# Final layer norm: weight multiplied during the output product, bias and mean added by a rank-two product

## The chip, the cores and the metric

The kernel runs on one core of a Trainium2 chip. The metric is the device time of one execution in microseconds (us), lower is better. The engines named below are TensorE (PE), VectorE (DVE), ScalarE (ACT), GpSimd (POOL) and the DMA queues that SyncE (SP) and GpSimd issue to.

## What is computed

One layer of a decoder trunk for 512 prompt tokens and 64 sample tokens, 2048 channels, all in float32. Only the last line concerns the change:

```python
def layer_norm(x, g, b):
    mu = jnp.mean(xf, axis=-1, keepdims=True)
    var = jnp.mean(jnp.square(xf - mu), axis=-1, keepdims=True)
    return (xf - mu) * lax.rsqrt(var + LN_EPS) * g + b

def mix_and_norm(x, y_a, o_b, z_b, g_a, g_b, w_o_a, w_o_b, w_out, ln_g, ln_b):
    ...
    return layer_norm(DN_ALPHA * x + merged @ w_out, ln_g, ln_b)
```

Everything before it (the input projection, attention, the gated branch) fills the first 2258 us of the kernel and is the same in both versions.

## The kernel before

The output product works on 16 blocks of 128 channels. For each block PE streams four quarters of the weight (`quarter`, L736, 96 records) into one of two PSUM banks (`acc`). Each quarter was rounded by ACT (`wh`, L942) and split by DVE (`wl`, L1231) two quarters ahead, through a ring of three. ACT then copies the block out (`read_out`, L1184), PE transposes it to tokens by channels (`out_turn`, L923 and L925, into `turn`), DVE adds the scaled input (`residual`, L1655), which fills 128 channels of `res`, and takes the statistics of that block (`statistics`, L1664). `res` holds 5 tiles of tokens: tiles 0 to 3 have 128 rows, tile 4 has the 64 sample rows.

After block 15 nothing but the norm is left. DVE aggregates the statistics (L1685), ACT takes the square root (L1198), DVE the reciprocal (L1689) and `shift`, minus the mean times the reciprocal (L1690). The normalisation itself then runs over ten half tiles of 1024 channels, in an order that is written out by hand. Tiles 0 and 1 are DVE's alone: `centred` (L1706, subtract the mean and multiply with the weight `lng`) and `scaled` (L1713, multiply with the reciprocal and add the bias `lnb`). Tiles 2, 3 and 4 go through three engines: ACT scales and shifts (L1204), DVE multiplies with the weight (`gain`, L1700), POOL adds the bias (L643). SP stores each half tile (L447) when it is done. All waits are on semaphores in program order, so an engine that waits holds everything behind it in its own queue.

In float32 a product whose operands are plain `F32` shows as two PE records in the trace; the operands rounded to `F32R` show as one. The transposes show as one.

Of the kernel before, what the change touches and what calls it, by code (L numbers as in the profile page):

```python
# [9 lines left out]
ALU = mybir.AluOpType  # L10
ACT = mybir.ActivationFunctionType

P = 128
D = 2048
# [3 lines left out]
SAMP = DEC_B * DEC_T  # L18
TOK = SEQ + SAMP
# [3 lines left out]
KB = D // P  # L23
# [102 lines left out]
    return N_TURN * (f - 1) + TURN_NAMES.index(name) + 1  # L126


def tile_rows(c):

    return P if c < 4 else SAMP


def half_cols(h):

    return slice(h * (D // 2), (h + 1) * (D // 2))


def build(nc, x_t, x_res, near_k, ones_k, units_k, cache_v, w_in, bias_t, w_st, w8_t, b_s, ln_v_g, ln_v_b, w_o_a, w_o_b,
# [11 lines left out]
    with ExitStack() as ctx:  # L151
        sem = lambda name: ctx.enter_context(nc.semaphore(name))
        top = 229344

        def sb(name, shape, at, dt=F32, end=top):
            assert at % 4 == 0 and at + 4 * int(np.prod(shape[1:])) <= end, (name, at)
            return nc.alloc_sbuf_tensor_at(name, list(shape), dt, offset=at)

        def row_of(at, end):
            place = [at]  # L160

            def put(name, *shape, dt=F32):
                size = -(-4 * int(np.prod(shape)) // 32) * 32
                place[0] += size
                return sb(name, (P,) + shape, place[0] - size, dt, end)
            return put

        base = 16512
        ident, bias, small = sb("ident", [P, P], base), sb("bias", [P, 136], base + 512), sb("small", [P, 32], base + 1056)
        QUAD = 4 * HK * HALF  # L170
        X1 = base + 1184
        FREE = X1 + 4 * QUAD
# [15 lines left out]
        put = row_of(R, top)  # L188
# [15 lines left out]
        put = row_of(FREE, X2)  # L204
# [12 lines left out]
        put = row_of(R2, top)  # L217
# [23 lines left out]
        put = row_of(R2, R)  # L241
# [1 line left out]
        gbuf = put("gbuf", 4, TOK)  # L243
        mtmp = put("mtmp", TOK)
        xn = sb("xn", [P, 2, 5, P], X2 + 3 * QUAD)
        rstat, rmv, shift = put("rstat", 5, KB, 6), put("rmv", 5, 2), put("shift", 5)
        put = row_of(R, top)
        vn = put("vn", 5, WIDTH)
        wct, bsb, w8 = put("wct", HEADS, P), put("bsb", HEADS, P), put("w8", HEADS, SAMP)
# [1 line left out]
        tri, tri8 = put("tri", P), put("tri8", SAMP)  # L251
        vstat, vmv = put("vstat", 5, 2, 6), put("vmv", 5, 2)
        mh, ml = sb("mh", [P, KB, TOK], X1, F32R), sb("ml", [P, KB, TOK], R, F32R)
        lng, lnb = sb("lng", [P, D], FREE), sb("lnb", [P, D], FREE + 8192)
        res = sb("res", [P, 5, D], FREE + 4 * QUAD)

        acc = ctx.enter_context(nc.psum_tensor("acc", [P, 2, 1024], F32))
        turn = ctx.enter_context(nc.psum_tensor("turn", [P, 2, 512], F32))
        scp = ctx.enter_context(nc.psum_tensor("scp", [P, 1024], F32))
# [45 lines left out]
        out_read_acc, out_turned, out_read = sem("out_read_acc"), sem("out_turned"), sem("out_read")  # L305
        xn_in = [sem("xn_in0"), sem("xn_in1")]
        ln_in, o_var, o_sqrt = sem("ln_in"), sem("o_var"), sem("o_sqrt")
        o_norm_v, o_norm_p, o_stored = sem("o_norm_v"), sem("o_norm_p"), sem("o_stored")
        o_gained, o_centred = sem("o_gained"), sem("o_centred")
        o_scaled, o_stats = sem("o_scaled"), sem("o_stats")  # L310

        block = ctx.enter_context(nc.Block())
        ds = bass.ds
# [1 line left out]
        def pair_cols(f, k):  # L315

            if k is None:
                return COL_VA + 2 * f * P, COL_VA + (2 * f + 1) * P
            first, second = ((0, COL_K), (COL_V, COL_V + WIDTH), (WIDTH, COL_K + WIDTH), (COL_V + 2 * WIDTH, COL_ZB),
                             (2 * WIDTH, COL_K + 2 * WIDTH), (COL_U, COL_ZA))[k]  # L320
            return first + f * P, second + f * P
# [23 lines left out]
        def _(sp):  # L345
# [4 lines left out]
            c1, c2 = pair_cols(0, None)  # L350
# [88 lines left out]
                for u in range(4):  # L439
                    load(Q_OUT + 4 * n + u, quarter_of(w_out, QB * u, n * P))  # L440

            for by, n in ((o_norm_p, 0), (o_norm_v, 0), (o_norm_p, 1), (o_norm_v, 1), (o_norm_p, 2), (o_norm_p, 3),
                          (o_norm_v, 2), (o_norm_p, 4), (o_norm_v, 3), (o_norm_p, 5)):
                c, cols = n // 2 + (2 if by is o_norm_p else 0), half_cols(n % 2)
                rows = tile_rows(c)
                sp.wait_ge(by, n + 1)
                sp.dma_start(y_out[c, 0:rows, cols], res[0:rows, c, cols]).then_inc(o_stored, 16)  # L447

            sp.wait_ge(s_stored[0], 96 * HEADS)
# [7 lines left out]
        def _(pool):  # L457
# [174 lines left out]
            residual(1)  # L632
            pool.wait_ge(m_split, KB)
            pool.dma_start(lng[:], ln_g.broadcast_to([P, D])).then_inc(ln_in, 16)
            pool.dma_start(lnb[:], ln_b.broadcast_to([P, D])).then_inc(ln_in, 16)
            for n in range(2, 16):
                pool.wait_ge(out_read, 2 * n - 2)
                residual(n)
            for n in range(6):
                c, cols = 2 + n // 2, half_cols(n % 2)  # L640
                t = res[0:tile_rows(c), c, cols]
                pool.wait_ge(o_gained, n + 1)
                pool.tensor_tensor(t, t, lnb[0:tile_rows(c), cols], ALU.add).then_inc(o_norm_p, 1)  # L643


        def pairs(pair):
# [13 lines left out]
        def _(pe):  # L660
# [275 lines left out]
                        out_turn(n - 1)  # L936
            out_turn(15)


        @block.scalar  # L940
        def _(act):
            copy = lambda out, src: nc.scalar.activation(out, src, ACT.Copy)  # L942
# [226 lines left out]
            for t in range(32):  # L1169
                ahead(Q_A + t)  # L1170
                n = t // 2
# [24 lines left out]
            read_out(15)  # L1196
            act.wait_ge(o_var, 1)
            nc.scalar.activation(rmv[:, :, 1], rmv[:, :, 1], ACT.Sqrt).then_inc(o_sqrt, 1)  # L1198
            for n in range(6):
                c, cols = 2 + n // 2, half_cols(n % 2)  # L1200
                t = res[0:tile_rows(c), c, cols]

                act.wait_ge(o_var, 2)
                nc.scalar.activation(t, t, ACT.Identity, bias=shift[0:tile_rows(c), c:c + 1],  # L1204
                                     scale=rmv[0:tile_rows(c), c, 1:2]).then_inc(o_scaled, 1)


        @block.vector
        def _(dve):
            v = nc.vector  # L1210

            class Links:

                n = 0
# [13 lines left out]
            links = Links()  # L1228
# [374 lines left out]
            for t in range(32):  # L1603
# [13 lines left out]
                if t == 7:  # L1617
                    links.then(v.memset(vmv[:], 1.0))
                    for c in range(5):
                        rows = tile_rows(c)  # L1620
# [29 lines left out]
            def residual(n):  # L1650

                dve.wait_ge(xn_in[n % 2], 16 * (n // 2 + 1))
                for part, (rows, c0, c1) in enumerate(((P, 0, 4), (SAMP, 4, 5))):
                    dve.wait_ge(out_turned, 2 * n + part + 1)
                    v.scalar_tensor_tensor(out=res[0:rows, c0:c1, n * P:(n + 1) * P], in0=xn[0:rows, n % 2, c0:c1, :],  # L1655
                                           scalar=ALPHA, in1=turn[0:rows, part, 0:(c1 - c0) * P]
                                           .rearrange("p (c d) -> p c d", d=P),
                                           op0=ALU.mult, op1=ALU.add).then_inc(out_read, 1)

            def statistics(n):  # L1660
                dve.wait_ge(out_read, 2 * n + 2)
                for c in range(5):
                    rows = tile_rows(c)
                    v.bn_stats(rstat[0:rows, c, n, :], res[0:rows, c, n * P:(n + 1) * P]).then_inc(o_stats, 1)  # L1664

            for n in range(16):
                for u in range(4):
                    q = Q_OUT + 4 * n + u
                    if n == 0 and u == 0:
                        merge(Q_A, 15, 16)  # L1670
                    if q + LEAD < Q_END:
                        ahead(q)
                    if n == 0 and u == 0:
                        split_m(15)
                    if n > 0 and u == 2:
                        residual(n - 1)
                    if n > 0 and u == 3:
                        statistics(n - 1)
            residual(15)
            statistics(15)  # L1680
            dve.wait_ge(o_stats, 5 * KB)
            links.then(v.memset(rmv[:], 1.0))
            for c in range(5):
                rows = tile_rows(c)
# [2 lines left out]
            v.tensor_scalar(rmv[:, :, 1], rmv[:, :, 1], LN_EPS, None, ALU.add).then_inc(o_var, 1)  # L1687
            dve.wait_ge(o_sqrt, 1)
            links.then(v.reciprocal(rmv[:, :, 1], rmv[:, :, 1]))  # L1689
            v.scalar_tensor_tensor(out=shift[:], in0=rmv[:, :, 0], scalar=-1.0, in1=rmv[:, :, 1],  # L1690
                                   op0=ALU.mult, op1=ALU.mult).then_inc(o_var, 1)
            dve.wait_ge(ln_in, 32)

            def gain(n):


                c, cols = 2 + n // 2, half_cols(n % 2)
                t = res[0:tile_rows(c), c, cols]
                dve.wait_ge(o_scaled, n + 1)
                v.tensor_tensor(t, t, lng[0:tile_rows(c), cols], ALU.mult).then_inc(o_gained, 1)  # L1700

            def centred(n):

                c, cols = n // 2, half_cols(n % 2)
                t = res[0:P, c, cols]
                v.scalar_tensor_tensor(out=t, in0=t, scalar=rmv[:, c, 0:1], in1=lng[:, cols],  # L1706
                                       op0=ALU.subtract, op1=ALU.mult).then_inc(o_centred, 1)

            def scaled(n):
                c, cols = n // 2, half_cols(n % 2)  # L1710
                t = res[0:P, c, cols]
                dve.wait_ge(o_centred, n + 1)
                v.scalar_tensor_tensor(out=t, in0=t, scalar=rmv[:, c, 1:2], in1=lnb[:, cols],  # L1713
                                       op0=ALU.mult, op1=ALU.add).then_inc(o_norm_v, 1)


            for step, n in ((centred, 0), (gain, 0), (gain, 1), (scaled, 0), (gain, 2), (centred, 1), (scaled, 1),
                            (gain, 3), (centred, 2), (scaled, 2), (gain, 4), (gain, 5), (centred, 3), (scaled, 3)):
                step(n)


def tables():
# [97 lines left out]
```

## Time and profile before

| | us |
|---|---|
| median of 3 runs | 2504.29 |
| lowest, highest | 2503.12, 2511.63 |
| the profiled execution, its own time | 2510.55 |
| its span, first to last instruction | 2508.9 |
| PE, DVE, ACT, POOL busy | 2306.7, 1611.3, 923.8, 265.0 |
| last PE record of the output product to the end of the span | 2467.5 to 2508.9 |

The span is what the views of the trace cover; the profiled execution's own time is 1.65 us above it. That execution is 6.3 us slower than the median of the runs, so a sum made in the trace is a difference that is then added to either.

### The profile page before, as it was taken

The page shows a single profiled execution, that of the slowest core. Times are in us where ns is not written, and L with a number is a line of the kernel's source. Part 1 is how long each engine was busy: PE and PEld are TensorE (multiplying, and loading weights), DVE is VectorE, ACT ScalarE, POOL GpSimd, SP SyncE. Part 2 cuts the span into 40 slices and gives each one's busy share as a digit, 9 for nine tenths or more (in the row PEclk, how much of TensorE's full clock was granted, in tenths as well). Part 3 has the DMA queues.
Part 4 walks back from the last instruction along what each step waited for, and adds up shares of the span by engine and source line. Part 5 has one row for each costly group of instructions (what it writes and reads, how often), then busy time and mean ns, then how long its engine had stood idle before and what let it go on. Part 6 is the DMA issues. An engine that isn't in the chain of part 4 may idle for free.

```text
span 2508.9 us, 44550 instructions
## 1 busy us (share of the span) xinstructions
PE 2306.7 (92%) x17744; PEld 2258.8 (90%) x17744; DVE 1611.3 (64%) x2085; ACT 923.8 (37%) x1326; POOL 265.0 (11%) x453
## 2 busy tenths in 40 slices
PE   5999999999999999999968978979889979999993
PEld 4999999999999999999957978978779879999993
DVE  7677877777778777787565655655565647553336
ACT  4544444444444444444322322322323333332221
POOL 0100000000000000000222121122121110000003
PEclk8999999999999999999988999989999989999996
DMA  4433443343334333443576566566666563344332
GB/s 145 135 117 117 119 132 100 118 122 115 112 118 130 110 112 118 131 123 118 174 231 207 147 217 201 163 194 192 171 203 179 153 191 119 123 123 146 101 106 89
DMA packets 400348, 358.94 MB, mean 143 GB/s; under 512 B 15664, under 2 KB 359744, under 8 KB 398368
## 3 DMA queue, kind: packets, MB, share of 16 engines
q1 hardware_dynamic: 363168, 206.28, 28.2%
q0 software_dynamic: 36992, 149.90, 18.2%
q8 instruction: 150, 2.46, 0.4%
q14 instruction: 38, 0.31, 0.0%
HBM read 309.74 MB, written 46.37 MB: 142 GB/s over the span
## 4 chain that ended last, share of the span: by engine, by line
PE 76%; DVE 10%; DMA 7%; issue 3%; ACT 1%; POOL 1%; SPq 0%; DVEq 0%; ACTq 0%; POOLq 0%
PE acc L682 46%; PE acc L736 23%; DMA ones<-in_ones_k 4%; DVE prod L1419 2%; DVE far L1420 2%; PE scp L819 2%; PE scp L792 1%; PE turn L756 1%; DMA cache<-in_cache_v 1%; DVE sc L1444 1%; PE turn L691 1%; DMA gbuf<-gate_rows 1%; ACT wh L942 1%; DVE wl L1231 1%; DVE sc L1441 1%
## 5 line engine op out<-in xcount | busy, mean ns | idle before, releaser
L682 PE MATMUL acc<-xh,wph 128*128 128x288 f32 x2912 | 868.3, 298 | 38.4 <-DVE wpl L1231 29.2
L682 PE MATMUL acc<-xl,wph 128*128 128x288 f32 x2912 | 860.3, 295 | 0.0
L682 PE MATMUL acc<-xh,wpl 128*128 128x288 f32 x2912 | 857.2, 294 | 0.0
L682 PEld LDWEIGHTS acc<-xh,wph 128*128 128x128 f32 x2912 | 547.0, 188 | 40.9 <-issue 23.2
L682 PEld LDWEIGHTS acc<-xh,wpl 128*128 128x128 f32 x2912 | 549.5, 189 | 0.0
L682 PEld LDWEIGHTS acc<-xl,wph 128*128 128x128 f32 x2912 | 548.1, 188 | 0.0
L1231 DVE TENSOR_TENSOR wl<-raw,wh 128x512 fp32r<-128x512 f32 x256 | 176.8, 691 | 417.2 <-ACT wh L942 416.6
L942 ACT ACTIVATE wh<-raw 128x512 fp32r<-128x512 f32 x256 | 161.0, 630 | 565.6 <-PE acc L736 463.5
L736 PE MATMUL acc<-xh,wh 128*128 128x288 f32 x1024 | 237.7, 314 | 8.9 <-DVE wl L1231 6.1
L736 PE MATMUL acc<-xl,wh 128*128 128x288 f32 x1024 | 224.4, 301 | 0.0
L736 PE MATMUL acc<-xh,wl 128*128 128x288 f32 x1024 | 223.9, 301 | 0.0
L1022 ACT ACTIVATE s<-acc,bias 128x288 f32<-128x288 f32 x208 | 98.7, 500 | 273.8 <-PE acc L682 249.5
L1231 DVE TENSOR_TENSOR wpl<-w_a,wph 128x1024 fp32r<-128x1024 f32 x104 | 127.4, 1225 | 83.1 <-ACT wph L942 81.5
L736 PEld LDWEIGHTS acc<-xh,wh 128*128 128x128 f32 x1024 | 166.5, 195 | 12.5 <-DVE wl L1231 6.5
L1231 DVE TENSOR_TENSOR wpl<-w_c,wph 128x1024 fp32r<-128x1024 f32 x104 | 127.2, 1223 | 73.5 <-ACT wph L942 72.8
L736 PEld LDWEIGHTS acc<-xl,wh 128*128 128x128 f32 x1024 | 169.6, 194 | 0.0
L942 ACT ACTIVATE wph<-w_a 128x1024 fp32r<-128x1024 f32 x104 | 110.1, 1059 | 160.4 <-DVE w_a L1254 160.4
L736 PEld LDWEIGHTS acc<-xh,wl 128*128 128x128 f32 x1024 | 169.2, 194 | 0.0
L942 ACT ACTIVATE wph<-w_c 128x1024 fp32r<-128x1024 f32 x104 | 109.8, 1056 | 66.3 <-PE acc L682 63.8
L736 PE MATMUL acc<-mh,wh 128*128 128x288 f32 x512 | 110.8, 298 | 0.0
L736 PE MATMUL acc<-mh,wl 128*128 128x288 f32 x512 | 109.7, 296 | 0.0
L736 PE MATMUL acc<-ml,wh 128*128 128x288 f32 x512 | 109.5, 295 | 0.0
(212 smaller groups left out, 3637.4 us busy)
## 6 DMA issues: line engine op xcount, KB each, us to landing
raw<-in_w_in SPq DMA_DIRECT2D x128, 256.0 KB, 5.0
cache<-in_cache_v POOLq DMA_DIRECT2D x64, 448.0 KB, 5.3
w_a<-in_w_in SPq DMA_DIRECT2D x52, 512.0 KB, 3.8
w_c<-in_w_in SPq DMA_DIRECT2D x52, 512.0 KB, 3.8
w_b<-in_w_in SPq DMA_DIRECT2D x52, 512.0 KB, 3.8
w_d<-in_w_in SPq DMA_DIRECT2D x52, 512.0 KB, 3.9
ones<-in_ones_k POOLq DMA_DIRECT2D x64, 256.0 KB, 3.2
raw<-in_w_out SPq DMA_DIRECT2D x64, 256.0 KB, 2.7
```

The costliest lines, as they stand in the source:

```text
L682: done = pe.matmul(bank, w[ring][:, k, :], a[x][:, k, :], start=(j in (0, 1, 3, 5) and k == 0 and t == 0), stop=(k == HK - 1 and t == 2), ...
L691: done = pe.transpose(turn[0:rows, b, c * P:(c + 1) * P], src, ident[:])
L736: done = pe.matmul(accv[p][:, h, :], w[:, q % RING, n, :], moving(k, h, low), start=(first and n == 0 and t == 0), stop=(last and n == QB ...
L756: done = pe.transpose(turn[0:width, n % 2, cols:cols + rows], src, ident[0:rows, 0:rows])
L792: pe.matmul(scp[:, 0:SEQ], qT[par][0][:, cols], kT[par][0][:, 0:SEQ], start=True, stop=True)
L819: done = pe.matmul(scp[0:DEC_T, b * P:(b + 1) * P], p[:, at:at + DEC_T], val, start=(n == 0 and t == 0), stop=(n == 6 and t == 2))
L942: copy = lambda out, src: nc.scalar.activation(out, src, ACT.Copy)
L1022: nc.scalar.activation(out[:], bank_x, ACT.Identity, bias=b, scale=sign).then_inc(s_copied, 1)
L1231: return v.tensor_tensor(out, src, hi.bitcast(F32), ALU.subtract)
L1419: links.then(v.tensor_tensor(prod[:], keys, rows.broadcast_to([P, 4, 2, P]), ALU.mult))
L1420: v.tensor_reduce(far_1[:, :, DEC_T * b:DEC_T * b + DEC_T], prod[:].rearrange("p j u (c d) -> p j (u c) d", d=32), mybir.AxisListType.X, A ...
L1441: v.tensor_scalar(tile, tile, small[0:rows, c + 1:c + 2], None, ALU.mult).then_inc(normed, 1)
```

## The change

The weight is multiplied into `res` block by block, right after the statistics of the block, on DVE (`gain(n)`, two instructions: four tiles of 128 rows in one, the 64 sample rows in the other). What is left after the last block is `res * r + (b - mean * r * g)`. The bracket is a product of rank two: a 2 x tokens matrix (`rows_x`: ones, and minus the mean times the reciprocal) against a 2 x 2048 matrix (`rows_gb`: bias and weight). DVE writes the pairs (`pairs_x`), PE turns them (five small transposes), ACT copies them out of PSUM to `rows_x`, and PE makes the bracket for each half tile as two products of 512 columns into one of three PSUM areas used in turn. For tiles 0 to 3 DVE finishes with one instruction that reads `res` and that area. For the sample tile PE also adds `res` times a diagonal matrix `diag` of the reciprocals, and ACT copies the sum out. POOL no longer computes, and the bias is loaded as one row where it was copied to 128 partitions.

```diff
+LAST_TILES = [(0, 0), (0, 1), (1, 0), (4, 0), (1, 1), (2, 0), (4, 1), (2, 1), (3, 0), (3, 1)]
...
 # POOL
-            pool.dma_start(lnb[:], ln_b.broadcast_to([P, D])).then_inc(ln_in, 16)
+            pool.dma_start(rows_gb[0:1, :], ln_b).then_inc(ln_in, 16)
+            pool.dma_start(rows_gb[1:2, :], ln_g).then_inc(ln_in, 16)
...
-            for n in range(6):
-                ...
-                pool.wait_ge(o_gained, n + 1)
-                pool.tensor_tensor(t, t, lnb[0:tile_rows(c), cols], ALU.add).then_inc(o_norm_p, 1)
 # PE
+            pe.wait_ge(o_var, 2)
+            for c in range(5):
+                done = pe.transpose(scp[0:2, c * P:c * P + tile_rows(c)], pairs_x[0:tile_rows(c), c, :],
+                                    ident[0:tile_rows(c), 0:tile_rows(c)])
+            done.then_inc(x_turned, 1)
+            pe.wait_ge(x_rows, 1)
+            pe.wait_ge(ln_in, 48)
+            for n, (c, half) in enumerate(LAST_TILES):
+                rows, bank = tile_rows(c), (acc[:, 0, :], acc[:, 1, :], scp)[n % 3]
+                if c == 4:
+                    pe.wait_ge(o_gained, 2 * KB)
+                if n >= 3:
+                    ...   # the reader of tile n - 3 is done
+                for i in range(2):
+                    cols = slice(half * (D // 2) + i * 512, half * (D // 2) + (i + 1) * 512)
+                    out = bank[0:rows, i * 512:(i + 1) * 512]
+                    done = pe.matmul(out, rows_x[0:2, c * P:c * P + rows], rows_gb[0:2, cols], start=True, stop=(c < 4))
+                    if c == 4:
+                        done = pe.matmul(out, diag[:], res[0:rows, c, cols], start=False, stop=True)
+                done.then_inc(o_ranked, 1)
 # ACT
-            for n in range(6):
-                ...
-                nc.scalar.activation(t, t, ACT.Identity, bias=shift[...], scale=rmv[...]).then_inc(o_scaled, 1)
+            act.wait_ge(x_turned, 1)
+            copy(rows_x[:], scp[0:2, 0:TOK]).then_inc(x_rows, 1)
+            for n, (c, half) in enumerate(LAST_TILES):
+                if c == 4:
+                    act.wait_ge(o_ranked, n + 1)
+                    copy(res[0:SAMP, 4, half_cols(half)], ...).then_inc(o_norm_a, 1)
 # DVE
+            def gain(n):
+                cols = slice(n * P, (n + 1) * P)
+                dve.wait_ge(o_stats, 5 * (n + 1))
+                ...
+                for rows, c0, c1 in ((P, 0, 4), (SAMP, 4, 5)):
+                    t = res[0:rows, c0:c1, cols]
+                    v.tensor_tensor(t, t, lng[0:rows, cols]..., ALU.mult).then_inc(o_gained, 1)
...
                     if n > 0 and u == 3:
                         statistics(n - 1)
+                        gain(n - 1)
...
+            links.mark(v.tensor_scalar(diag[:], ident[0:SAMP, 0:SAMP], rmv[0:SAMP, 4, 1:2], None, ALU.mult))
-            for step, n in ((centred, 0), (gain, 0), (gain, 1), (scaled, 0), ...):
-                step(n)
+            gain(15)
+            for n, (c, half) in enumerate(LAST_TILES):
+                if c < 4:
+                    t = res[0:P, c, half_cols(half)]
+                    dve.wait_ge(o_ranked, n + 1)
+                    v.scalar_tensor_tensor(out=t, in0=t, scalar=rmv[:, c, 1:2], in1=..., op0=ALU.mult, op1=ALU.add).then_inc(o_norm_v, 1)
```

DVE's row inside the output product, one block, before:

```order
L1231 TENSOR_TENSOR wl<-raw,wh 128x512 [waits w_round]
L1664 BN_STATS rstat<-res 128x6 [waits out_read]
L1664 BN_STATS rstat<-res 128x6 x3
L1664 BN_STATS rstat<-res 64x6
L1231 TENSOR_TENSOR wl<-raw,wh 128x512 [waits w_round] x3
```

The same place in the changed kernel, where the line numbers are some 30 higher:

```order
L1262 TENSOR_TENSOR wl<-raw,wh 128x512 [waits w_round]
L1695 BN_STATS rstat<-res 128x6 [waits out_read]
L1695 BN_STATS rstat<-res 128x6 x3
L1695 BN_STATS rstat<-res 64x6
L1705 TENSOR_TENSOR res<-res,lng 128x4x128 [waits o_stats]
L1705 TENSOR_TENSOR res<-res,lng 64x128
L1262 TENSOR_TENSOR wl<-raw,wh 128x512 [waits w_round] x3
```

The two products with the weight now stand between the statistics and the next split of a quarter.

DVE's row behind the last statistics, before:

```order
L1689 RECIPROCAL rmv<-rmv 128x5 [waits o_sqrt]
L1690 SCALAR_TENSOR_TENSOR shift<-rmv 128x5 [waits vector_done]
L1706 SCALAR_TENSOR_TENSOR res<-res,rmv,lng 128x1024 [waits ln_in]
L1700 TENSOR_TENSOR res<-res,lng 128x1024 [waits o_scaled] x2
L1713 SCALAR_TENSOR_TENSOR res<-res,rmv,lnb 128x1024 [waits o_centred]
L1700 TENSOR_TENSOR res<-res,lng 128x1024 [waits o_scaled]
...
```

The same place in the changed kernel:

```order
L1733 RECIPROCAL rmv<-rmv 128x5 [waits o_sqrt]
L1734 TENSOR_SCALAR diag<-ident,rmv 64x64 [waits vector_done]
L1735 SCALAR_TENSOR_TENSOR pairs_x<-rmv 128x5
L1705 TENSOR_TENSOR res<-res,lng 128x4x128 [waits o_stats]
L1705 TENSOR_TENSOR res<-res,lng 64x128
L1745 SCALAR_TENSOR_TENSOR res<-res,rmv,acc 128x1024 [waits o_ranked,vector_done,o_gained]
L1745 SCALAR_TENSOR_TENSOR res<-res,rmv,acc 128x1024 [waits o_ranked]
...
```

Fourteen instructions over 1024 channels became eight, and each of the eight waits for PE.

PE's row behind the last transposes of the product, where before there was nothing:

```order
L931 MATMUL turn<-ident,ostage 64x128
L947 MATMUL scp<-ident,pairs_x 2x128 [waits o_var]
L947 MATMUL scp<-ident,pairs_x 2x128 x3
L947 MATMUL scp<-ident,pairs_x 2x64
L965 MATMUL acc<-rows_gb,rows_x 128x512 [waits ln_in,x_rows]
L965 MATMUL acc<-rows_gb,rows_x 128x512 x3
L965 MATMUL scp<-rows_gb,rows_x 128x512 x2
L965 MATMUL acc<-rows_gb,rows_x 64x512 [waits o_norm_v,o_gained]
L967 MATMUL acc<-res,diag 64x512
L965 MATMUL acc<-rows_gb,rows_x 64x512
L967 MATMUL acc<-res,diag 64x512
```

In all there are 20 products with `rows_gb` and 4 with `diag`, each of 512 columns, in plain `F32`.

## Rows read from the trace of the kernel before

**Rows 1.** The chain that ended last, behind the output product: start, us, what.
```profile
2467.56 0.66 ACT ostage L1184
...
2468.27 0.66 PE turn L923 x4
...
2474.24 0.18 DVE shift L1690
...
2474.45 1.25 ACT res L1204
...
2500.32 3.25 DVE res L1713
```

**Rows 2.** Groups of DVE by form, 2474 to 2504 us: busy us, mean ns, idle before.
```profile
L1713 DVE SCALAR_TENSOR_TENSOR res<-res,rmv,lnb 128x1024 f32<-128x1024 f32 x4 | 13.1, 3279 | 0.1
L1706 DVE SCALAR_TENSOR_TENSOR res<-res,rmv,lng 128x1024 f32<-128x1024 f32 x4 | 7.2, 1795 | 0.0
L1700 DVE TENSOR_TENSOR res<-res,lng 128x1024 f32<-128x1024 f32 x4 | 6.9, 1753 | 0.1
L1700 DVE TENSOR_TENSOR res<-res,lng 64x1024 f32<-64x1024 f32 x2 | 2.3, 1209 | 0.0
```

**Rows 3.** Readers of the weight's tile `lng`: ns min/median/max, first and last start.
```profile
L1706 DVE SCALAR_TENSOR_TENSOR res<-res,rmv,lng x4: 1273/1276/3353, 2474.3 to 2496.9; 128x1024 f32<-128x1024 f32 x4
```

**Rows 4.** Last stretches: busy of PE, PEld, DVE, ACT, POOL (records); PEclk granted, DMA share, GB/s.
```profile
2474.42:2503.57 29.15, 0.00 (x0) 0.00 (x0) 28.93 (x14) 6.90 (x6) 19.70 (x6) 0.50 0.35 135
2503.57:2508.90 5.33, 0.00 (x0) 0.00 (x0) 0.00 (x0) 0.00 (x0) 0.00 (x0) 0.50 0.46 148
```

**Rows 5.** Timeline of DVE in one block: start, us, instruction, idle before and releaser.
```profile
2452.37 1.05 DVE L1664 BATCH_NORM_STATS2 rstat<-res 128x6 f32<-128x128 f32 x5
2454.96 0.69 DVE L1231 TENSOR_TENSOR wl<-raw,wh 128x512 fp32r<-128x512 f32 x1 [1.54 <-ACT wh L942]
```

**Rows 6.** Groups of DVE by form over the output product.
```profile
L1231 DVE TENSOR_TENSOR wl<-raw,wh 128x512 fp32r<-128x512 f32 x60 | 41.6, 693 | 133.4 <-ACT wh L942 133.4
...
L1655 DVE SCALAR_TENSOR_TENSOR res<-xn,turn 64x128 f32<-64x128 f32 x16 | 4.4, 273 | 0.0
...
L1687 DVE TENSOR_SCALAR rmv<-rmv 128x5 f32<-128x5 f32 x1 | 0.2, 172 | 0.0
```

**Rows 7.** Timeline of PE: plain float32 records of 512 columns, at two times.
```profile
1267.12 2.07 PE L792 MATMUL scp<-qkv 128*128 128x512 f32 x2 [6.28 <-DVE small L1444]
1268.98 0.42 PE L794 MATMUL scp<-qkv 128*128 128x128 f32 x1
...
1959.65 1.02 PE L792 MATMUL scp<-qkv 128*128 128x512 f32 x2
1960.51 0.61 PE L794 MATMUL scp<-qkv 128*128 128x128 f32 x4
```

**Rows 8.** Earlier stretches, columns as in rows 4.
```profile
1340.80:1344.80 4.00, 4.00 (x47) 3.87 (x43) 3.96 (x6) 0.00 (x0) 0.13 (x1) 1.00 0.02 4
1344.80:1346.90 2.10, 1.50 (x16) 1.28 (x14) 0.69 (x1) 0.00 (x0) 0.41 (x1) 1.00 0.45 117
1347.60:1350.90 3.30, 3.30 (x16) 3.30 (x15) 1.99 (x3) 1.26 (x2) 2.79 (x6) 0.50 0.55 135
1301.20:1306.50 5.30, 1.79 (x9) 1.12 (x9) 4.87 (x7) 1.50 (x3) 1.41 (x3) 1.00 0.56 162
1306.50:1310.00 3.50, 3.50 (x29) 3.44 (x28) 2.51 (x8) 1.03 (x2) 1.64 (x4) 1.00 0.79 224
1267.10:1272.10 5.00, 4.98 (x16) 3.95 (x17) 1.92 (x7) 0.49 (x1) 0.42 (x1) 0.50 1.03 390
1272.50:1275.50 3.00, 2.62 (x20) 2.39 (x18) 0.00 (x0) 0.77 (x3) 0.00 (x0) 1.00 1.04 382
```

**Rows 9.** Groups of PE by form, 1344.8 to 1346.9 us; "64*128" is array rows*columns.
```profile
L826 PE MATMUL scp<-psn,qkv 64*128 64x64 f32 x6 | 0.9, 280 | 0.6 <-DVE osm L1535 0.6
L829 PE MATMUL scp<-ident,osm 8*128 8x8 f32 x8 | 0.7, 204 | 0.0
```

More of the change, by code:

```diff
@@ L126, in turn_no, with last_no @@
     return N_TURN * (f - 1) + TURN_NAMES.index(name) + 1
+LAST_TILES = [(0, 0), (0, 1), (1, 0), (4, 0), (1, 1), (2, 0), (4, 1), (2, 1), (3, 0), (3, 1)]
+def last_no(n):
+    return sum(c < 4 for c, _ in LAST_TILES[:n + 1])
 def tile_rows(c):
@@ L245, in build @@
         xn = sb("xn", [P, 2, 5, P], X2 + 3 * QUAD)
-        rstat, rmv, shift = put("rstat", 5, KB, 6), put("rmv", 5, 2), put("shift", 5)
+        rstat, rmv = put("rstat", 5, KB, 6), put("rmv", 5, 2)
         put = row_of(R, top)
@@ L253, in build @@
         mh, ml = sb("mh", [P, KB, TOK], X1, F32R), sb("ml", [P, KB, TOK], R, F32R)
-        lng, lnb = sb("lng", [P, D], FREE), sb("lnb", [P, D], FREE + 8192)
+        lng, rows_gb, rows_x = sb("lng", [P, D], FREE), sb("rows_gb", [2, D], FREE + 8192), sb("rows_x", [2, TOK], FREE + 16384)
+        pairs_x, diag = sb("pairs_x", [P, 5, 2], FREE + 18688), sb("diag", [SAMP, SAMP], FREE + 18752)
         res = sb("res", [P, 5, D], FREE + 4 * QUAD)
@@ L307, in build @@
         ln_in, o_var, o_sqrt = sem("ln_in"), sem("o_var"), sem("o_sqrt")
-        o_norm_v, o_norm_p, o_stored = sem("o_norm_v"), sem("o_norm_p"), sem("o_stored")
-        o_gained, o_centred = sem("o_gained"), sem("o_centred")
-        o_scaled, o_stats = sem("o_scaled"), sem("o_stats")
+        o_norm_v, o_norm_a, o_stored = sem("o_norm_v"), sem("o_norm_a"), sem("o_stored")
+        o_gained, o_stats = sem("o_gained"), sem("o_stats")
+        x_turned, x_rows, o_ranked = sem("x_turned"), sem("x_rows"), sem("o_ranked")
         block = ctx.enter_context(nc.Block())
@@ L440, in _ @@
                     load(Q_OUT + 4 * n + u, quarter_of(w_out, QB * u, n * P))
[L442 to L446, printed above, removed]
+            for n, (c, half) in enumerate(LAST_TILES):
+                rows, cols = tile_rows(c), half_cols(half)
+                if c == 4:
+                    sp.wait_ge(o_norm_a, half + 1)
+                else:
+                    sp.wait_ge(o_norm_v, last_no(n))
                 sp.dma_start(y_out[c, 0:rows, cols], res[0:rows, c, cols]).then_inc(o_stored, 16)
@@ L638, in _ @@
                 residual(n)
-            for n in range(6):
-                c, cols = 2 + n // 2, half_cols(n % 2)
-                t = res[0:tile_rows(c), c, cols]
-                pool.wait_ge(o_gained, n + 1)
-                pool.tensor_tensor(t, t, lnb[0:tile_rows(c), cols], ALU.add).then_inc(o_norm_p, 1)
         def pairs(pair):
@@ L937, in _ @@
             out_turn(15)
+            pe.wait_ge(o_var, 2)
[10 more added lines that the diff above has]
+                if n >= 3:
+                    cb, hb = LAST_TILES[n - 3]
+                    if cb == 4:
+                        pe.wait_ge(o_norm_a, hb + 1)
+                    else:
+                        pe.wait_ge(o_norm_v, last_no(n - 3))
+                for i in range(2):
[5 more added lines that the diff above has]
+                done.then_inc(o_ranked, 1)
         @block.scalar
@@ L1198, in _ @@
             nc.scalar.activation(rmv[:, :, 1], rmv[:, :, 1], ACT.Sqrt).then_inc(o_sqrt, 1)
-            for n in range(6):
[L1200 to L1205, printed above, removed]
+            act.wait_ge(x_turned, 1)
+            copy(rows_x[:], scp[0:2, 0:TOK]).then_inc(x_rows, 1)
+            for n, (c, half) in enumerate(LAST_TILES):
+                if c == 4:
+                    act.wait_ge(o_ranked, n + 1)
+                    copy(res[0:SAMP, 4, half_cols(half)], (acc[0:SAMP, 0, :], acc[0:SAMP, 1, :], scp[0:SAMP, :])[n % 3]
+                         ).then_inc(o_norm_a, 1)
         @block.vector
@@ L1664, in statistics @@
                     v.bn_stats(rstat[0:rows, c, n, :], res[0:rows, c, n * P:(n + 1) * P]).then_inc(o_stats, 1)
+            def gain(n):
+                cols = slice(n * P, (n + 1) * P)
+                dve.wait_ge(o_stats, 5 * (n + 1))
+                if n == 0:
+                    dve.wait_ge(ln_in, 48)
+                for rows, c0, c1 in ((P, 0, 4), (SAMP, 4, 5)):
+                    t = res[0:rows, c0:c1, cols]
+                    v.tensor_tensor(t, t, lng[0:rows, cols].rearrange("p (o d) -> p o d", o=1)
+                                    .broadcast_to([rows, c1 - c0, P]), ALU.mult).then_inc(o_gained, 1)
             for n in range(16):
@@ L1678, in _ @@
                         statistics(n - 1)
+                        gain(n - 1)
+            links.then(v.memset(pairs_x[:], 1.0))
             residual(15)
@@ L1689, in _ @@
             links.then(v.reciprocal(rmv[:, :, 1], rmv[:, :, 1]))
-            v.scalar_tensor_tensor(out=shift[:], in0=rmv[:, :, 0], scalar=-1.0, in1=rmv[:, :, 1],
+            links.mark(v.tensor_scalar(diag[:], ident[0:SAMP, 0:SAMP], rmv[0:SAMP, 4, 1:2], None, ALU.mult))
+            v.scalar_tensor_tensor(out=pairs_x[:, :, 1], in0=rmv[:, :, 0], scalar=-1.0, in1=rmv[:, :, 1],
                                    op0=ALU.mult, op1=ALU.mult).then_inc(o_var, 1)
[L1692 to L1718, printed above, removed]
-                step(n)
+            gain(15)
+            dve.wait_ge(o_gained, 2 * KB)
+            links.wait()
+            for n, (c, half) in enumerate(LAST_TILES):
+                if c < 4:
+                    t = res[0:P, c, half_cols(half)]
+                    dve.wait_ge(o_ranked, n + 1)
+                    v.scalar_tensor_tensor(out=t, in0=t, scalar=rmv[:, c, 1:2],
+                                           in1=(acc[:, 0, :], acc[:, 1, :], scp[:])[n % 3],
+                                           op0=ALU.mult, op1=ALU.add).then_inc(o_norm_v, 1)
 def tables():
```

## The prediction

> **What bounds the kernel now.** I read the chain that ended last first, and of it only what follows the output product, since nothing earlier changes except on DVE. After the last block the chain is one line of dependent steps: copy out, transpose, residual, statistics, square root, `shift` at 2474.24, and then the norm, which ends with a DVE instruction at 2500.32 plus 3.25, so at 2503.57 [rows 1]. The stretches say what works in between: from 2474.42 to 2503.57 DVE is busy 28.93 of 29.15 us, POOL 19.70, ACT 6.90, and PE not at all, with a granted clock of 0.50, which is 1.2 GHz [rows 4]. Then come 5.33 us in which only stores run. So the norm is DVE's 14 instructions, and the place where a change can act is 29.15 us long.
>
> The groups of DVE by form show why it is 29 and not 18: the same instruction over 1024 channels takes 1.21 to 1.28 us in some cases and 3.3 in others (L1713 3279 ns mean, L1706 from 1273 to 3353) [rows 2, 3]. The long ones lie beside POOL's additions. Fourteen times about 1.25 would be 17.5, so some 11.5 us are lost to that.
>
> **What the change removes.** All 14 DVE instructions, 13.1 + 7.2 + 6.9 + 2.3 = 29.5 us of rows [rows 2], with POOL's and ACT's share of the norm.
>
> **What it adds to DVE inside the product.** Per block one multiplication over 128x512 (nearest row: 693 ns, the same size with two SBUF inputs) and one over 64x128 (nearest: 273 ns, the same shape, another operation) [rows 6], 0.97 us. They stand behind the statistics, in front of the next `wl`, and that one is preceded by 1.54 us of waiting for ACT [rows 5]. So 0.57 us of cover are left and I price the 15 blocks at nothing. Were the cover gone, `wl` would slip, and what waits for it is PE, which works two quarters behind; a slip of some tenths is not passed on. The last block's pair (0.97 us) runs while PE turns the pairs, also at nothing.
>
> **The new chain, from 2474.42.**
> - `diag`, one more instruction on DVE before the pairs: 172 ns for 5 elements [rows 6], somewhat more for 64, taken as 0.25. Bounds 0.17 and 0.7 (a 512-element row).
> - Five transposes on PE. Four of the same width took 0.66 us at full clock [rows 1]; here the clock is 0.50, so up to 1.5; I take 1.3.
> - ACT's copy of 2x576 to `rows_x`: 0.66 as for 128x576 [rows 1]. PE can start at 2474.42 + 0.25 + 1.3 + 0.66 + 0.1 for handing over = 2476.7.
> - The products. 20 rank-two ones and 4 with `diag` make 24, and a plain float32 product is two records, so 48 records of 512 columns. The trace has such records: two of them took 0.86 us to the next start at full clock, and 1.86 us at half [rows 7]. That is 0.43 and 0.93 each; the 0.93 includes the start after a wait, so for a dense run at half clock I take twice 0.43, 0.86.
> - DVE's last instruction. 1.28 us, from the short ones of [rows 3]; it reads PSUM now, which `residual` does without being slower per element. DVE needs 8 x 1.28 = 10.2 us in all, ACT two copies, so PE with its 48 records is the bound of the norm at either clock: 20.6 us at full, 41.3 at half. With three PSUM areas in turn it never waits for their readers.
>
> **The decision: which clock.** The sum hangs on whether PE is granted full speed while it makes products whose stationary operand fills 2 of the 128 rows of the array. Before no such product exists, so the nearest rows decide. The clock usually comes back when PE works densely: from 1267.1 PE was busy 4.98 of 5.00 us at 0.50, and had 1.00 afterwards; from 1347.6 it had 0.50 for at least 3.30 us of full work [rows 8]. Those were products of all 128 rows. The other observation is how it fell at 1347: PE worked without a gap until 1344.8, was busy 1.50 of the next 2.10 us, mostly with products of 64 and 8 rows (L826, L829) [rows 9], went back to full work, and had 0.50 all the same. From 1301.2, with products of 128 rows, it was busy only 1.79 of 5.30 us, and kept 1.00 [rows 8]. Less work of full rows kept the clock, more work of few rows did not. I read this as: products of few rows do not hold or raise the clock as full ones do. Then a run with 2 rows of 128 does not raise it, and the norm stays at half speed. This is thin evidence, one fall against one hold, and I give it 6 in 10.
>
> The Trainium skill (TensorE: Matmul & The Clock Gate, Part 1, Terms) says that the gate goes by how busy PE has been, and names no dependence on rows. By that rule the dense stream of products would be granted 2.4 GHz after its first few us, and the change would come out a little faster; that is the first rival below.
>
> **Sum at half clock.** 2476.7 + 48 x 0.86 = 2518.0; 0.35 until the last result is there (a record's 1.2 less its 0.86, from the 2.07 of [rows 7]); 1.28 for DVE: 2519.6. Before it was 2503.57, so plus 16.1. The stores behind it stay 5.3 us. The profiled execution would go from 2510.55 to 2526.6 and the median from 2504.29 to 2520.4. Bounds of this case: 0.93 for a record adds 3.4 (2523.8); 0.85, the transposes at 0.8 and a shorter hand-over take off 1.5 (2518.9).
>
> **Rivals.**
> - *The clock rises during the products* (0.31). For: every dense run of full products in the trace raised it, and PE has no gap here. Against: [rows 8, 9] as above. After 3.3 to 5.4 us of half clock (the two stretches of [rows 8]), which cost half of themselves, the norm's PE time is 20.6 + 2.2 = 22.8, so DVE ends at 2476.7 + 22.8 + 0.2 + 1.28 = 2501.0: minus 2.6, a median of 2501.7. Its own range is 2500 to 2504. This is the case on the other side: 2476.7 + 20.6 + half of the slow time + 1.5 reaches 2503.57 when 9.5 us run at half clock, so a rise before that decides.
> - *The clock rises for a part* (0.06). The sample tiles' products with `diag` have 64 rows; if they lift it for some us, each us at full saves one at half. With 3 to 8 us of it the median is 2512 to 2517.
> - *DVE becomes late in the product* (0.03). If the weight's product takes 1.9 us or more instead of 0.97, for instance beside POOL's issue of a transfer, the cover is gone and up to 0.4 us per block could reach PE: 15 x 0.4 = 6, on top of either case. Against: in the product POOL only issues transfers, once a block.
>
> **How the numbers follow.** Half clock 0.60, rising 0.31, partly 0.06, late DVE 0.03. The likeliest gives 2520. A measurement of this kernel tells about 0.5% from no change, 12.5 us here. Half clock is 16.1 us, 0.64%, so most of it, 0.5, is slower by over 0.5% and 0.1 falls within, by a smaller record or the scatter of the runs; the rising case is within, at 0.1% faster. That makes 0.02 faster, 0.47 same, 0.51 slower. The range takes in both cases, 2500 to 2524; half clock alone has 2516 to 2524.
>
> **What the profile after would show.** PE records with `rows_gb` 0.86 us apart from the first to the last and a granted clock of 0.50 until the end would show the decision right; 0.43 apart from the third tile on would show it wrong. DVE's eight last instructions at about 1.3 us, each idle before for `acc` or `scp`, show PE as the bound. The first `rows_gb` record near 2.3 us after the pairs tests the hand-over. Inside the product the wait of the third `wl` behind `gain` should be near 0.6 us; PE's time per block should not change. Wrong too would be a record count other than 48.

## The result and the profile after

The changed kernel takes 2523.69 us in the median of 4 runs (2516.78 to 2525.56), the kernel before 2506.67 (2503.12 to 2511.63, 4 runs). The ratio is 1.0061, with a 95% interval of 1.0033 to 1.0089: 0.61% of 2506.67 is 15.3 us more; the two medians by themselves differ by 17.0. The forecast was 16.1 us more, a median of 2520.4, and its range for half clock was 2516 to 2524, so the measured median lies inside it close to its upper end.

The profiled execution of the changed kernel is the fastest of its four (2516.78, span 2514.8). Its span is only 5.9 us above that of before, so the first thing is to see which part of it differs. The list of what reads the product's operand `mh` gives the first and last start of the output product's records in both kernels, before and after:

```profile
L736 PE MATMUL acc<-mh,wl x512: 292/295/302, 2255.1 to 2467.2; 128*128 128x288 f32 x171
```

```profile
L742 PE MATMUL acc<-mh,wl x512: 292/295/303, 2245.5 to 2457.6; 128*128 128x288 f32 x171
```

The product lasts 212.1 us in both, so the weight's multiplications inside it cost nothing. It begins 9.6 us earlier in the changed kernel's execution. The stages ahead are the same in both, so this is put down to the scatter between executions. What the change acts on is the stretch from the last record of the product to the end of the span: 2508.9 - 2467.2 = 41.7 us before, 2514.8 - 2457.6 = 57.2 after, 15.5 more. This stretch is compared below too.

The chain that ended last, in the changed kernel, from the pairs on (start, us, what):

```profile
2464.64 0.24 DVE diag L1734
2464.89 0.08 DVE pairs_x L1735
...
2465.02 1.22 PE scp L947 x5
...
2466.26 0.65 ACT rows_x L973
...
2466.95 7.19 PE acc L965 x8
2474.14 3.41 PE scp L965 x4
2477.55 1.89 PE acc L965 x2
2479.45 1.89 PE acc L967 x2
...
2506.94 3.43 PE acc L965 x4
...
2510.39 1.28 DVE res L1745
```

Where [rows 1] has DVE up to the last instruction, there are now 43.4 us of PE without a break. Four records of one width take 3.41, 0.853 each. The stretches of the same kernel, columns as in [rows 4], for that run of PE and for the stores behind it:

```profile
2466.95:2510.37 43.42, 43.40 (x48) 12.38 (x48) 8.96 (x7) 2.03 (x2) 0.00 (x0) 0.50 0.26 97
2511.67:2514.80 3.13, 0.00 (x0) 0.00 (x0) 0.00 (x1) 0.00 (x0) 0.00 (x0) 0.50 0.40 168
```

PE is busy 43.40 of 43.42 us with 48 records, and the clock granted is 0.50 throughout; DVE is busy 8.96. The timeline of DVE shows it waiting for PE in front of each of its instructions, which take 1.28 us each with an operand in PSUM. Three of them:

```profile
2474.18 1.28 DVE L1745 SCALAR_TENSOR_TENSOR res<-res,rmv,acc 128x1024 f32<-128x1024 f32 x1 [2.02 <-PE acc L965]
2477.59 1.28 DVE L1745 SCALAR_TENSOR_TENSOR res<-res,rmv,scp 128x1024 f32<-128x1024 f32 x1 [2.13 <-PE scp L965]
2488.87 1.28 DVE L1745 SCALAR_TENSOR_TENSOR res<-res,rmv,acc 128x1024 f32<-128x1024 f32 x1 [10.00 <-PE acc L965]
```

And one block inside the product, beside [rows 5]: the two multiplications take 0.89 us, and 0.62 us of waiting for ACT are left in front of the next split.

```profile
2429.41 1.05 DVE L1695 BATCH_NORM_STATS2 rstat<-res 128x6 f32<-128x128 f32 x5
2430.49 0.89 DVE L1705 TENSOR_TENSOR res<-res,lng 128x512 f32<-128x512 f32 x2
2432.00 0.69 DVE L1262 TENSOR_TENSOR wl<-raw,wh 128x512 fp32r<-128x512 f32 x1 [0.62 <-ACT wh L973]
```

### The profile page after: what moved, and what is told of

The parts are those of the page before. It is cut to its first block, busy times and chain, and to the rows that moved or that the text cites. A ratio compares the mean times of both kernels' runs of the same rounds, so it can differ in the third digit from the quotient of the medians.

```text
span 2514.8 us, 44679 instructions
## 1 busy us (share of the span) xinstructions
PE 2350.4 (93%) x17797; PEld 2272.0 (90%) x17797; DVE 1606.7 (64%) x2113; ACT 918.4 (37%) x1323; POOL 244.9 (10%) x448
## 4 chain that ended last, share of the span: by engine, by line
PE 79%; DVE 9%; DMA 7%; issue 3%; ACT 1%; POOL 1%; SPq 0%; DVEq 0%; ACTq 0%; POOLq 0%
PE acc L688 45%; PE acc L742 23%; DMA ones<-in_ones_k 5%; PE scp L825 3%; DVE prod L1450 2%; DVE far L1451 2%; PE scp L798 1%; PE turn L762 1%; PE acc L965 1%; DVE sc L1475 1%; PE turn L697 1%; DMA gbuf<-gate_rows 1%; ACT wh L973 1%; DVE sc L1472 1%; PE scp L810 1%
```

## The experiments

The profile shows that PE bounds the norm at half clock. It does not show why the clock stays there. Theory A is the prediction's: products that fill few rows of the array do not raise it. Theory B is the rival: something else keeps it down, the idle stretch ahead, plain float32, or the data.

**Filling the rows.** The two operands get 128 rows, 126 of them zeros. GpSimd makes the zeros early in the output product.

```diff
-        rows_gb, rows_x = sb("rows_gb", [2, D], FREE + 8192), sb("rows_x", [2, TOK], FREE + 16384)
+        rows_gb, rows_x = sb("rows_gb", [P, D], FREE + 8192), sb("rows_x", [P, TOK], FREE + 16384)
+            pool.memset(rows_gb[:], 0.0).then_inc(padded, 1)
+            pool.memset(rows_x[:], 0.0).then_inc(padded, 1)
...
-                    done = pe.matmul(out, rows_x[0:2, c * P:c * P + rows], rows_gb[0:2, cols], ...)
+                    done = pe.matmul(out, rows_x[0:128, c * P:c * P + rows], rows_gb[0:128, cols], ...)
...
+            copy(rows_x[0:2, :], scp[0:2, 0:TOK]).then_inc(x_rows, 1)
```

> The changed kernel with its two operands rows_x and rows_gb padded with zeros to 128 rows, so that each product fills all rows of the array; columns, count and results are the same (two zero fills on GpSimd early in the output product are added). Theory A (products of few rows do not raise the clock): the granted clock goes to 1.00 some 3 to 5 us after the first padded product, the records then stand 0.43 us apart where they stood 0.86, the norm gets 16 to 19 us shorter than in the changed kernel, and the kernel is about 3 us faster than before, ratio 0.999, within 0.997 to 1.001. Theory B (the clock stayed at half because the stream begins after an idle stretch, or because plain float32 products or mostly zero data do not count): granted clock 0.50 to the end, ratio 1.006 as for the change.

Measured: 2503.42 us in the median of 12 runs, ratio to before 0.9985 (0.9975 to 0.9995). The clock rose 5.9 us after the first padded product. Stretches of this kernel, and two rows of its timeline of PE, in front of the rise and behind it:

```profile
2473.67:2479.50 5.83, 5.83 (x7) 2.52 (x8) 1.28 (x1) 0.00 (x0) 0.00 (x0) 0.50 0.00 0
2479.60:2499.06 19.46, 19.45 (x42) 5.91 (x40) 7.68 (x6) 2.04 (x2) 0.00 (x0) 1.00 0.51 188
```

```profile
2473.67 6.67 PE L968 MATMUL acc<-rows_gb,rows_x 128*128 128x512 f32 x8 [0.73 <-ACT rows_x L976]
2480.18 1.88 PE L968 MATMUL scp<-rows_gb,rows_x 128*128 128x512 f32 x4
```

The same 48 records take 25.4 us instead of 43.4, and the stretch behind the product is 39.5 us, 17.7 less than in the changed kernel. Nothing but the number of rows differs in these products: they are still plain float32, they still follow the idle stretch, and their data are now mostly zeros. None of these three keeps the clock down, and theory A holds. Rows of zeros count here; no run filled them with other numbers.

**Half of the rows.** The same kernel with 64 for 128 in the product:

```diff
-                    done = pe.matmul(out, rows_x[0:128, c * P:c * P + rows], rows_gb[0:128, cols], ...)
+                    done = pe.matmul(out, rows_x[0:64, c * P:c * P + rows], rows_gb[0:64, cols], ...)
```

> The same with 64 rows instead of 128. Theory A in a graded form (each row counts): half of the rows is too little, the clock stays at 0.50 and the records stay 0.86 us apart. Theory A with a step (some rows suffice): it rises as with 128 rows. Theory B: 0.50 here and with 128 rows.

Measured: one run of 2519.79 us, and the clock stayed down. The groups of PE behind the pairs, and the stretch:

```profile
L968 PE MATMUL acc<-rows_gb,rows_x 64*128 64x512 f32 x20 | 18.4, 1081 | 0.7 <-ACT rows_x L976 0.7
```

```profile
2471.01:2513.31 42.30, 42.28 (x48) 13.43 (x48) 8.97 (x7) 2.03 (x2) 0.00 (x0) 0.50 0.27 99
```

PE busy 42.28 of 42.30 us with 64 rows has 0.50 to the end. So 64 rows do not suffice. Whether each row counts, or a step lies between 64 and 128, this run does not tell. The 1.1 us by which it is shorter than the 43.42 of the changed kernel has its own reason: where products of 2 rows and of 64 rows alternate there, each pair of records takes 1.89 us; here all have 64, and the chain of this kernel shows 1.71.

**A warm start.** The changed kernel with products of 128 rows that nobody reads, in front of the pairs:

```diff
             out_turn(15)
+            for i in range(46):
+                pe.matmul(accv[0][:, 0, :], wh[:, 0, i % QB, :], mh[:, i % KB, 0:HALF], start=True, stop=True)
             pe.wait_ge(o_var, 2)
```

> The changed kernel, with 46 products of 128 rows and 288 columns that nobody reads put on TensorE between the last transposes of the output product and the pairs, so that the clock is at 1.00 when the products of 2 rows begin. Theory A: the clock falls to 0.50 within some us although TensorE never pauses, and the norm is only 2 to 4 us shorter than in the changed kernel. Theory B (an idle stretch ahead is what keeps it low): the clock holds 1.00 to the end, and the norm is about 20 us shorter.

Measured: one run of 2518.84 us; the stretch behind the product is 54.2 us, 3.0 less than in the changed kernel. The stretches with the filler products, then the products of 2 rows:

```profile
2464.50:2470.56 6.06, 6.06 (x49) 5.99 (x48) 5.55 (x18) 0.69 (x2) 0.00 (x0) 1.00 0.00 0
2471.87:2474.70 2.83, 2.83 (x7) 1.36 (x8) 0.70 (x1) 0.00 (x0) 0.00 (x0) 1.00 0.00 0
2474.90:2478.00 3.10, 3.10 (x5) 1.30 (x4) 1.66 (x2) 0.00 (x0) 0.00 (x0) 0.50 0.43 165
2478.00:2512.42 34.42, 34.41 (x38) 8.59 (x37) 6.41 (x5) 2.03 (x2) 0.00 (x0) 0.50 0.29 107
```

The products of 2 rows begin at 2.4 GHz, PE is busy all the time from the first of them, and some 3 us later the clock falls to 1.2. In front of the first of them are 1.31 us in which PE was busy only 0.58. That short pause is not what holds the clock down: the kernel before kept 1.00 with PE busy 1.79 of 5.30 us, on products of 128 rows [rows 8], and here the clock does not come back in the 37 us of unbroken work that follow. So such products neither raise the clock nor hold it, and the idle stretch ahead is not the reason.

**Without the diagonal products.** From the kernel with 128 rows, the sample tile is finished by DVE like the others:

```diff
-                    if c == 4:
-                        done = pe.matmul(out, diag[:], res[0:rows, c, cols], start=False, stop=True)
...
-                if c < 4:
-                    t = res[0:P, c, half_cols(half)]
+                rows = tile_rows(c)
+                t = res[0:rows, c, half_cols(half)]
```

> Kernel e1 in which VectorE finishes the sample tile like the others, so that the 4 products with diag, the diag instruction and the two copies on ScalarE are gone: 40 records instead of 48, and 10 instead of 8 instructions of 1.28 us on VectorE. Theory A with TensorE as the bound at either clock: 8 records of 0.43 us less than e1, and no change of tile width next to a diag product, so 3.5 to 5 us faster than e1, about 7 us faster than before, ratio 0.997. If the clock stays at 0.50: 7 to 8 us less than the change, ratio 1.003. If VectorE has become the bound (12.8 us of work), less than 2 us faster than e1.

Measured: 2498.85 us in 9 runs, ratio 0.9966 (0.9955 to 0.9977), 4.6 us under the kernel with 128 rows. The clock rose 4 us after the first product:

```profile
2471.10:2475.10 4.00, 4.00 (x5) 1.85 (x6) 0.07 (x1) 0.00 (x0) 0.00 (x0) 0.50 0.00 0
2475.10:2491.25 16.15, 16.14 (x36) 5.71 (x34) 11.43 (x9) 0.00 (x0) 0.00 (x0) 1.00 0.62 227
```

PE is busy 20.14 of 20.15 us, so it is still the bound at 2.4 GHz, as expected. The stretch behind the product is 34.1 us, 5.4 less than with 128 rows and `diag`.

**The bias on DVE instead of GpSimd.** This goes back to the kernel before and tests the other reading, that GpSimd's additions made DVE's instructions long. GpSimd's loop is left out, and DVE does the six additions:

```diff
-            for n in range(6):
-                ...
-                pool.tensor_tensor(t, t, lnb[0:tile_rows(c), cols], ALU.add).then_inc(o_norm_p, 1)
+            def added(n):
+                ...
+                v.tensor_tensor(t, t, lnb[0:tile_rows(c), cols], ALU.add).then_inc(o_norm_p, 1)
-            for step, n in ((centred, 0), (gain, 0), (gain, 1), (scaled, 0), ...):
+            for step, n in ((centred, 0), (gain, 0), (gain, 1), (added, 0), (scaled, 0), (gain, 2), (added, 1), ...):
```

> The kernel before, with GpSimd's six additions of the bias given to VectorE, which then has 20 instructions over 1024 channels instead of 14. The prediction's reading that 11.5 us of the norm before were lost to instructions that ran beside GpSimd's: none is longer than 1.3 us now, the norm takes 20 times 1.25 = 25 us instead of 29.15, and the kernel is 4 us faster than before, ratio 0.998. If the long instructions had another cause (their own operands, the stores), they stay at 3.3 us in part and the norm takes over 35 us, ratio above 1.002.

Measured: 2499.47 us in 7 runs, ratio 0.9969 (0.9958 to 0.9980), 7.8 us faster than before, where 4 were expected. Groups of DVE by form, beside [rows 2]:

```profile
L1714 DVE SCALAR_TENSOR_TENSOR res<-res,rmv,lnb 128x1024 f32<-128x1024 f32 x4 | 5.1, 1281 | 0.0
L1707 DVE SCALAR_TENSOR_TENSOR res<-res,rmv,lng 128x1024 f32<-128x1024 f32 x4 | 5.1, 1280 | 0.0
L1701 DVE TENSOR_TENSOR res<-res,lnb 128x1024 f32<-128x1024 f32 x4 | 4.9, 1220 | 0.0
L1695 DVE TENSOR_TENSOR res<-res,lng 128x1024 f32<-128x1024 f32 x4 | 4.8, 1221 | 0.1
```

The same multiplication and addition that took 3279 ns beside GpSimd takes 1281 alone. Twenty instructions end earlier than fourteen did. The size was off for two reasons. The instructions overlap a little at their ends: in the chain each counts 1.13 to 1.20 us, and the norm takes 23.4 us (2470.75 to 2494.13) where 25 were expected, 5.8 less than the 29.15 before. And the stores behind it took 4.3 us where they had taken 5.3; the cause of that is not shown.

**One pass instead of four.** From the kernel without diagonal products. The plain float32 product is two records of two cycles per column (0.853 us at 1.2 GHz is 1024 cycles for 512 columns). Here bias, weight and scaled mean are split into a rounded part and a rest, and all partial products stand in different rows of one operand of 128 rows, so that 512 columns are one record. The split of bias and weight is made inside the product, on ACT and DVE.

```diff
...
+            for at in (0, 32, 64):
+                pool.dma_start(rows_gb[at:at + 1, :], ln_b).then_inc(ln_in, 16)
+                pool.dma_start(rows_gb[at + 1:at + 2, :], ln_g).then_inc(ln_in, 16)
...
+                        copy(rows_m[:, cols], rows_gb[:, cols]).then_inc(gb_round, 1)                              # ACT
+                        low(rows_m[32:34, cols], rows_gb[32:34, cols], rows_m[32:34, cols]).then_inc(gb_split, 1)  # DVE
...
+            # pairs_x: columns 0, 32 ones; 1, 33 the scaled mean; 65 its rest behind rounding; zeros elsewhere
...
-                    done = pe.matmul(out, rows_x[0:128, c * P:c * P + rows], rows_gb[0:128, cols], start=True, stop=True)
+                    done = pe.matmul(out, rows_x[:, c * P:c * P + rows], rows_m[:, cols], start=True, stop=True)
```

> Kernel e4 with the product of bias and mean in one pass: bias, weight and scaled mean are split into a rounded part and a rest, as the kernel does with its other operands, and the five partial products stand in different rows of one 128-row operand, so that each 512 columns are one record of one cycle per column. 20 records of 0.43 us at half clock instead of 40 of 0.86. TensorE then needs 8.6 us at half clock, less than VectorE's ten instructions of 1.28, so VectorE bounds the norm and the clock no longer matters: its last instruction ends some 16.5 us after the pairs are ready where e4 has 23.4, with 0.5 us more for the split of the mean, so 6 to 7 us faster than e4 and 14 us faster than before, ratio 0.994. If TensorE or the hand-over of PSUM areas still bounds, the gain over e4 is less than 3 us.

Measured: 2491.46 us in 5 runs, ratio 0.9945 (0.9931 to 0.9959), the fastest of all. The medians put it 7.4 us under the kernel without diagonal products, but the two were measured beside different sets of runs of the kernel before. Their ratios to it, 0.9945 and 0.9966, are 5.3 us apart, and their stretches behind the product 6.3. The end of its chain, and the stretch:

```profile
2471.79 1.24 PE acc L961 x2
...
2473.16 9.62 DVE res L1748 x8
2482.78 1.19 DVEq L159
2483.97 1.19 DVE res L1748
```

```profile
2471.79:2485.16 13.37, 8.85 (x20) 4.21 (x20) 12.00 (x10) 0.00 (x0) 0.00 (x0) 0.76 0.72 254
```

PE is busy 8.85 of 13.37 us and DVE 12.00. DVE runs its ten instructions without a wait, so it is the bound again. The clock decides little more than when the first pair of records is done (1.24 us): at half clock two records take 0.85 us here (starts at 2473.66 and 2474.51), so all 20 would take 8.5, still less than DVE's 12.00. The stretch behind the product is 27.8 us, against 41.7 before and 57.2 in the changed kernel.

## Why the prediction was right

- *What bounded the norm before.* Right in kind: DVE's instructions, made long by GpSimd's. Shown by taking GpSimd away (3279 to 1281 ns). The 11.5 us put down to it were a little low: 14 instructions at the 1.17 us that one counts without GpSimd (23.38 us for 20) are 16.4 us, so 12.8 of the 29.15 were lost. The Trainium skill (GPSIMD Engine Reference, Specifications) says that GpSimd shares its SBUF interfaces with VectorE and contends with its instructions of two SBUF inputs. The trace agrees: 3279 ns beside GpSimd's additions, 1281 without them.
- *The weight inside the product.* Right: 0.89 us for a pair (forecast 0.97), 0.62 us of cover left (0.57), the product 212.1 us in both.
- *The new chain up to the first product.* A little shorter than forecast. The 2.3 us were counted from the end of `shift`, which is 2.5 from the end of the reciprocal (2474.22 before). In the changed kernel the reciprocal ends at 2464.62 and the first product starts at 2466.95, 2.33 later, and 1.98 behind the pairs, which end at 2464.97. The pairs added 0.08 to the chain where `shift` had 0.18. `diag` was 0.24, the transposes 1.22 (1.3), the copy 0.65 (0.66).
- *The clock.* Right, and from thin evidence, one fall and one hold [rows 8]. The runs showed it: 2 rows stay at 0.50, 64 rows too, 128 rows rise to 1.00, and a clock that is up falls under products of 2 rows. The Trainium skill (TensorE: Matmul & The Clock Gate, Terms and Part 1) lets the gate go by how busy PE is. Here PE was busy 43.40 of 43.42 us and had 1.2 GHz, so the measurement decides against a rule that leaves out the rows.
- *The sum.* Two terms were off by some 2 us each and cancelled, so that 15.5 us in the trace came so near the forecast 16.1 is in part luck. PE's run was forecast as 41.3 plus 0.35 and took 43.4, 1.8 more. Of that 48 x 0.853 = 40.9, and most of the rest is the change of width, which the forecast did not have: 1.89 us for a pair of records where products of 2 and 64 rows alternate, and 3.71 for four where the columns go from 64 back to 128, against 1.71 and 3.41. The stores behind the last instruction were forecast as unchanged at 5.3 us and took 3.1, 2.2 less. With 0.2 less for the chain up to the first product, that makes the 0.6 us between 16.1 and 15.5. The timeline of SP has a likely reason for the stores; before, and in the changed kernel:

```profile
2503.60 0.85 SPq L447 DMA_DIRECT2D out_y<-res  x2
```

```profile
2511.70 0.33 SPq L457 DMA_DIRECT2D out_y<-res  x1
```

Before, the store of the last sample half, which GpSimd had finished at 2502.48, stood in SP's order behind that of DVE's last tile, so two stores were issued after 2503.57; now it is one. No run changed the order alone. The five kernels with one store behind the last instruction (the changed one, 128 rows, 64 rows, warm start, no diagonal) took 3.1 to 3.5 us for it, the kernel with the bias on DVE, which has the old order and two stores, 4.3. So two stores cost more, but by how much stays open.
- *The rivals.* The rise of the clock was put at minus 2.6 us against before. The kernel with 128 rows is that case: minus 3.8 us (ratio 0.9985), within its range of 2500 to 2504 against 2504.29. The same two terms cancelled there: PE's run was 25.4 us where 22.8 were forecast, the stores 3.4 where 5.3 were. The partial rise by the 64-row products did not come, and DVE was not late.

What stays open is how the clock goes between 64 and 128 rows, and whether rows of a larger operand and of a smaller one would count alike; only the two operands together were changed. The kernels with 64 rows and with the warm start ran once each; the granted clock is read from their traces.

## What to carry to other kernels

A small product at the end of a kernel, behind an idle stretch, begins at half clock: with 128 rows it stayed there for 4.0 and 5.9 us here, with 2 or 64 rows to its end, over 42 us. Filling the rows with zeros left the cost per record the same at either clock (0.853 and 0.43 us) and gave 18 us. Write plain float32 products of tiny rank as one pass, with the partial products of a split stacked in unused rows; that gave about another 6 us over the kernel without diagonal products, and took the bound from PE, and with it most of the clock's weight. And before work is moved to TensorE to relieve VectorE, look at why VectorE is slow: leaving out GpSimd's help alone gave 7.8 us, where moving the work to TensorE with products of 2 rows lost 15.

## What had not been expected

- A product next to one of another number of rows or columns costs more: a pair of records 1.89 us instead of 1.71 at half clock, and at full clock 1.00 instead of 0.86 in the kernel with 128 rows.
- The stores behind DVE's last instruction, which no one had meant to change, took 3.1 us in the changed kernel and 5.3 before. Part of it is likely their order: one store was left to issue in place of two.
- The output product takes 212.1 us to the tenth in both kernels, while its start moved by 9.6 us between two executions. A comparison of spans would have given 5.9 us, the stretch behind the product 15.5, and the runs 15.3.
